# A trunk with fp32 weights split into a high and a low part: the split done per unit or per half unit

## The chip, the cores and the metric

The kernel runs on one core of a Trainium2 chip. The metric is the device time of one execution in microseconds: the median of repeated runs.

## The reference

`reference(x, ...)` is a small encoder trunk on x of 1 x 256 x 2048 in fp32, with two layers. Layer 0's mixer projects to 5120 columns and feeds a bidirectional gated linear recurrence (RG-LRU, 16 blocks, width-4 convolution, GeLU gate) and a dilated sliding-window attention with 16 heads; both are concatenated and projected back. Layer 1's mixer is a differential attention: projection to 6144 columns, two softmax maps per head, their difference weights the values, RMS norm per head, projection back. After each mixer comes a SwiGLU FFN, `(silu(h @ w_gate) * (h @ w_up)) @ w_down`, with 5632 hidden columns. Each sub-layer has an RMS norm ahead and one behind, `x = x + rms_norm(m, gain)`. All weights are fp32, 2048 rows or more, and are read once.

## The kernel before

*Matmuls.* The 256 tokens are two row tiles (t = 0, 1). All dense products are cut into **units**: a unit is a block of 512 x 512 of a weight, four k-tiles of 128 rows (KT = 4). There are 384 units, numbered u. To be near fp32 precision with the fast float32r matmul, weights and activations are split into a rounded high part and the remainder: each of the two products of a unit (`product`, L956) runs three passes of four matmuls: w_hi with h_hi, then w_lo with h_hi, then w_hi with h_lo (h the activations). A unit is 2 x 3 x 4 = 24 matmuls of 128 x 128 by 512 columns.

*The path of a weight.* SP issues one load of 1 MB into one of three `raw` buffers (`load`, L621), as soon as the subtraction that last read that buffer is done. ACT rounds it to `w_hi` (four buffers; `hi`, L728), DVE subtracts, `w_lo = raw - w_hi` (three buffers; `lo`, L1139). Two semaphores count units, `hi_done` and `lo_done`; PE waits for them at the head of passes 0 and 1 (L963, L971), and tells with `unit_done` that a unit's buffers are free. ACT's rounding runs 3 units ahead of PE (HI_LEAD), DVE's subtraction 2 (LO_LEAD). Unit 0 alone is loaded, rounded and subtracted in halves of two k-tiles, with semaphores of its own (first_landed, first_hi, first_lo), so that the kernel starts sooner.

*Order.* Every engine walks the same list of tasks (`Plan`, `run`, L247; hand-written orders at the boundaries between sub-layers, L288 and L314), each picking its own; an engine's queue is in order, so that a wait holds up what stands behind it. In the recurrence of layer 0, ACT (tanh, exp, sqrt) and DVE (scans and products) have the gates' work between roundings and subtractions. The FFN blocks 1 to 10 of each layer are a peeled body and a hardware loop of nine (`body` on each engine, L1120 for PE), 12 units each: there the counts that are waited for are computed from the loop's register `it`.

The SP queue also carries the recurrence's small weights (L651), parameters, gains and the input chunks of x.

Of the kernel before, what the change touches and what calls it, by code (L numbers as in the profile page):

```python
# [31 lines left out]
P = 128  # L32
# [400 lines left out]
def trunk(nc, x, norm_mix_pre, norm_mix_post, norm_ffn_pre, norm_ffn_post,  # L433
# [9 lines left out]
    with ExitStack() as ctx:  # L443
# [68 lines left out]
        pv = ctx.enter_context(nc.psum_tensor("pv", [P, 2, T], F32))  # L512


        landed = [sem(f"landed{i}") for i in range(RAW)]
        first_landed = sem("first_landed")
        first_hi = sem("first_hi")
        first_lo = sem("first_lo")
        hi_done = sem("hi_done")
        lo_done = sem("lo_done")  # L520
        half_done = sem("half_done")
# [55 lines left out]
        block = ctx.enter_context(nc.Block())  # L577


        def wait_event(eng, e):  # L580

            eng.wait_ge(tp_free[e % 2], e // 2 + 1)
# [30 lines left out]

        @block.sync
        def _(sp):
            def load_first(src):

                for ks, landed_half in ((slice(0, KT // 2), first_landed), (slice(KT // 2, KT), landed[0])):
                    sp.dma_start(raw[0][:, ks, :], src.rearrange("(k p) n -> p k n", p=P)[:, ks, :]).then_inc(landed_half, 16)

            def load(u, src, it=0):  # L621

                if u >= RAW:
                    sp.wait_ge(lo_done, u - RAW + 1 + 12 * it)
                sp.dma_start(raw[u % RAW][:, :, :], src.rearrange("(k p) n -> p k n", p=P)).then_inc(landed[u % RAW], 16)

            def input_chunk(c):

# [35 lines left out]
            def load_slot(slot):  # L664
                block = NF - 1 if slot.w == "down" else slot.kg
                rows = slice(block * KC, (block + 1) * KC)
                src = weights[slot.w][slot.layer][rows, slot.cb * KC:(slot.cb + 1) * KC]
                if slot.u:
                    load(slot.u, src)
                else:  # L670
                    input_chunk(0)
                    sp.dma_start(pre[:, :, :], pre_T).then_inc(pre_in, 16)
                    sp.dma_start(ident[:, :], identity).then_inc(ident_in, 16)
                    load_first(src)

            def task_of(task):
                if task.kind == "half" and task.t == 0 and task.passes[0] == 0:
# [38 lines left out]

        @block.scalar
        def _(act):
            def first_half():

                act.wait_ge(first_landed, 16)
                act.activation(w_hi[0][:, 0:KT // 2, :], raw[0][:, 0:KT // 2, :], ACT.Copy).then_inc(first_hi, 1)

            def rest_of_first():
                act.wait_ge(landed[0], 16)
                act.activation(w_hi[0][:, KT // 2:KT, :], raw[0][:, KT // 2:KT, :], ACT.Copy).then_inc(hi_done, 1)

            def hi(u, it=0):  # L728
                act.wait_ge(landed[u % RAW], 16 * (u // RAW + 1) + 16 * (12 // RAW) * it)
                if u >= HI:  # L730
                    act.wait_ge(unit_done, u - HI + 1 + 12 * it)
                act.activation(w_hi[u % HI][:, :, :], raw[u % RAW][:, :, :], ACT.Copy).then_inc(hi_done, 1)  # L732

            def square(task):

# [157 lines left out]
            def task_of(task):  # L893
                if task.kind == "T":
                    transposed(task)
                elif task.kind in ("square", "y_square"):
                    square(task)
                elif task.kind == "hi":
                    hi(task.u) if task.u else rest_of_first()
                elif task.kind == "first_half":  # L900
                    first_half()
                elif task.kind == "silu":
                    act.wait_ge(rstd_done, task.stat + 1)
                    silu(task.n, task.u, lambda t: act.wait_ge(tp_done, task.stage_free[t] + 1))
                elif task.kind == "par":
                    parameters(task.i)
                elif task.kind == "evac":
                    evac(task)
                elif task.kind == "s":
                    softmax(task)  # L910
                elif task.kind == "pt":
                    prob_transposed(task)
                elif task.kind == "pv":
                    values(task)
                elif task.kind == "rg_gates":
                    gates(task.i)
                elif task.kind == "rg_root":
                    root(task.i)
                elif task.kind == "rg_out":
                    recurrence_hi(task.i)  # L920
# [34 lines left out]
        def _(pe):  # L955
            def product(u, n, lhs, first, last, t, passes=(0, 3), it=0, high=None, low=None):  # L956

                hi_tile, lo_tile = w_hi[u % HI], w_lo[u % LO]
                for j in range(*passes):
                    a, w = ((1, hi_tile), (1, lo_tile), (0, hi_tile))[j]  # L960
                    if j == 0:
                        if u:
                            pe.wait_ge(hi_done, u + 1 + 12 * it)  # L963
                        else:
                            pe.wait_ge(first_hi, 1)
                        if first and n >= 2:
                            pe.wait_ge(acc_free[n % 2][t], n // 2 + 3 * it)
                        if high:
                            pe.wait_ge(*high)
                    elif j == 1:  # L970
                        if u:  # L971
                            pe.wait_ge(lo_done, u + 1 + 12 * it)
                        else:
                            pe.wait_ge(first_lo, 1)
                    elif low:
                        pe.wait_ge(*low)
                    for k in range(KT):
                        if u == 0 and k == KT // 2 and j < 2:
                            pe.wait_ge(lo_done if j else hi_done, 1)
                        mm = pe.matmul(acc[n % 2][t][:, :], operand(lhs, a, k, t), w[:, k, :],  # L980
                                       start=first and k == 0 and j == 0, stop=last and k == KT - 1 and j == 2)
                if passes[1] == 3:
                    mm.then_inc(unit_done if t else half_done, 1)
# [147 lines left out]

        @block.vector
        def _(dve):
            def lo_first(ks):

                dve.tensor_tensor(w_lo[0][:, ks, :], raw[0][:, ks, :], w_hi[0][:, ks, :].bitcast(F32),
                                  ALU.subtract).then_inc(lo_done if ks.start else first_lo, 1)

            def lo(u, it=0):  # L1139
                dve.wait_ge(hi_done, u + 1 + 12 * it)  # L1140
                if u >= LO:
                    dve.wait_ge(unit_done, u - LO + 1 + 12 * it)
                dve.tensor_tensor(w_lo[u % LO][:, :, :], raw[u % RAW][:, :, :],  # L1143
                                  w_hi[u % HI][:, :, :].bitcast(F32), ALU.subtract).then_inc(lo_done, 1)

            def operand_lo(e, m, hi_ap, lo_ap, it=0):
                dve.wait_ge(t_hi, m + 1 + NT * it)
# [150 lines left out]
            def task_of(task):  # L1298
# [9 lines left out]
                elif task.kind in ("rms_x", "rms_y"):  # L1308
                    mean(task)
                elif task.kind == "lo":  # L1310
                    if task.u:
                        lo(task.u)
                    else:
                        dve.wait_ge(hi_done, 1)
                        lo_first(slice(KT // 2, KT))
                elif task.kind == "first_half":
                    dve.wait_ge(first_hi, 1)
                    lo_first(slice(0, KT // 2))
                elif task.kind == "add_output":
                    slot = task.slot  # L1320
                    if slot.w == "ev_out" and slot.starts:
                        dve.wait_ge(rg_out, RG_OUT * AT)
                    add_output(slot.n, slot.u, slot.cb, slot.starts, task.t)
                elif task.kind == "difference":
                    difference(task)
                elif task.kind == "heads_scale":
                    heads_scale(task.g)
                elif task.kind == "gate_up":
                    gate_up(task.n, task.n + 1, task.u, lambda t: dve.wait_ge(tp_done, task.tok_free[t] + 1))
                elif task.kind == "s":  # L1330
                    softmax(task)
                elif task.kind == "heads":
                    heads_mean(task.g)
                elif task.kind == "pv":
                    values(task)
                elif task.kind == "rg_gates":
                    decay(task.i)
                elif task.kind == "rg_scan":
                    scan(task.i)
                elif task.kind == "rg_out":  # L1340
                    recurrence_lo(task.i)
                elif task.kind == "par":
                    parameters(task.i)
# [222 lines left out]
```

## Time and profile before

| | us |
|---|---|
| median of 3 runs | 2288.51 |
| lowest, highest | 2287.97, 2291.24 |
| the profiled execution | 2291.3 |
| its span (first to last instruction) | 2289.2 |
| PE busy | 2253.2 (98%) |
| DVE busy | 1313.1 (57%) |
| ACT busy | 1049.7 (46%) |
| 16 DMA engines, mean busy share | 54.9% |

Busy time is the time in which an engine runs an instruction, waits left out. L980 is the matmul line, with 9216 of PE's 10273 matmuls. A matmul is on record with 389 ns, but the next one starts 227 ns after it, since they are pipelined; distances between starts tell the pace. The line numbers are those of the kernel before.

### The profile page before, as it was taken

How to read it: one execution, taken by the hardware profiler on the slowest of the kernel's cores; microseconds unless marked ns; L12 is line 12 of the kernel's file. 1: busy time of each engine (PE TensorE's matmuls, PEld its weight loads, DVE VectorE, ACT ScalarE, POOL GpSimd, SP SyncE). 2: the span in 40 equal slices, each digit the busy share in tenths (PEclk: the TensorE clock that was granted, in tenths of full speed). 3: DMA queues.
4: the chain of work that ended last, by engine and by line, in shares of the span. 5: the costliest groups of instructions: out<-in, count | busy, mean ns of one | idle time of the engine just before them, and what ended most of it. 6: DMA issues, size and time to landing. Idle time of an engine off the chain costs nothing.

```text
span 2289.2 us, 27425 instructions
## 1 busy us (share of the span) xinstructions
PE 2253.2 (98%) x10273; PEld 1857.8 (81%) x10273; DVE 1313.1 (57%) x1416; ACT 1049.7 (46%) x1231; POOL 173.0 (8%) x200
## 2 busy tenths in 40 slices
PE   8999999999999999999999999999999999999997
PEld 6887888888888888888787778788888888888886
DVE  5567467654554555545745555776554555555546
ACT  6677545543433433334555555546333433333332
POOL 0841001000000000000121001010000000000002
PEclk9999999999999999999999999999999999999999
DMA  7555444655555556555464545456555655556552
GB/s 256 170 165 175 146 146 150 214 188 190 196 185 193 192 184 195 189 186 197 148 203 147 165 148 166 166 166 203 198 188 186 199 184 193 191 183 198 187 193 101
DMA packets 211400, 413.71 MB, mean 181 GB/s; under 512 B 12072, under 2 KB 12672, under 8 KB 210816
## 3 DMA queue, kind: packets, MB, share of 16 engines
q1 hardware_dynamic: 211328, 412.75, 54.9%
q8 instruction: 45, 0.74, 0.1%
q14 instruction: 27, 0.22, 0.0%
HBM read 410.63 MB, written 2.10 MB: 180 GB/s over the span
## 4 chain that ended last, share of the span: by engine, by line
PE 59%; issue 33%; DVE 4%; ACT 2%; DMA 1%; POOL 1%; SPq 0%; DVEq 0%; ACTq 0%; POOLq 0%
PE acc L980 54%; PE tp L994 2%; DVE w_lo L1143 2%; PE sc L1068 1%; DMA raw<-in_ev_w_in 1%; PE pv L1092 1%; PE sc L1064 1%; PE pv L1097 1%; DVE xs L1183 0%; DMA gq<-in_norm_ffn_post 0%; POOL yacc L1441 0%; ACT w_hi L732 0%; DVE h_lo L1156 0%; DVE gq L1287 0%; DVE tok L1263 0%
## 5 line engine op out<-in xcount | busy, mean ns | idle before, releaser
L1143 DVE TENSOR_TENSOR w_lo<-raw,w_hi 128x2048 fp32r<-128x2048 f32 x383 | 880.7, 2301 | 491.5 <-PE acc L980 464.5
L732 ACT ACTIVATE w_hi<-raw 128x2048 fp32r<-128x2048 f32 x383 | 734.4, 1918 | 757.4 <-PE acc L980 728.0
L980 PE MATMUL acc<-w_hi,h_hi 128*128 128x512 f32 x2240 | 612.8, 395 | 7.6 <-ACT h_hi L779 7.6
L980 PE MATMUL acc<-w_lo,h_hi 128*128 128x512 f32 x2240 | 600.7, 390 | 3.4 <-DVE w_lo L1143 3.4
L980 PE MATMUL acc<-w_hi,h_lo 128*128 128x512 f32 x2240 | 600.0, 390 | 1.5 <-DVE h_lo L1156 1.5
L980 PEld LDWEIGHTS acc<-w_lo,h_hi 128*128 128x128 f32 x2240 | 421.0, 188 | 93.3 <-DVE w_lo L1143 4.7
L980 PEld LDWEIGHTS acc<-w_hi,h_lo 128*128 128x128 f32 x2240 | 419.9, 188 | 90.7 <-DVE h_lo L1156 3.2
L980 PEld LDWEIGHTS acc<-w_hi,h_hi 128*128 128x128 f32 x2240 | 414.7, 188 | 92.1 <-issue 10.7
L1200 DVE TENSOR_TENSOR yacc<-acc,yacc 128x512 f32<-128x512 f32 x208 | 141.7, 687 | 167.6 <-PE acc L980 167.6
L980 PE MATMUL acc<-w_hi,y_hi 128*128 128x512 f32 x832 | 224.5, 392 | 0.7 <-ACT y_hi L933 0.7
L980 PE MATMUL acc<-w_lo,y_hi 128*128 128x512 f32 x832 | 222.6, 389 | 0.0
L980 PE MATMUL acc<-w_hi,y_lo 128*128 128x512 f32 x832 | 222.5, 389 | 0.0
L980 PEld LDWEIGHTS acc<-w_lo,y_hi 128*128 128x128 f32 x832 | 156.2, 188 | 32.7
L980 PEld LDWEIGHTS acc<-w_hi,y_lo 128*128 128x128 f32 x832 | 156.2, 188 | 32.6
L980 PEld LDWEIGHTS acc<-w_hi,y_hi 128*128 128x128 f32 x832 | 155.1, 188 | 32.9 <-issue 1.6
L1441 POOL TENSOR_TENSOR yacc<-yacc,gq 128x512 f32<-128x512 f32 x20 | 33.0, 1667 | 1539.9 <-ACT junk L748 1539.9
L840 ACT ACTIVATE probT<-tp 128x256 f32<-128x256 f32 (+1 forms) x48 | 21.9, 456 | 116.2 <-PE pv L1097 64.9
L933 ACT ACTIVATE y_hi<-tp 128x512 fp32r<-128x512 f32 x44 | 24.1, 596 | 87.8 <-PE tp L994 87.8
L1393 DVE SCALAR_TENSOR_TENSOR tok<-acc,small,stage 128x512 f32<-128x512 f32 x44 | 33.0, 751 | 52.8 <-PE acc L980 52.8
L927 ACT ACTIVATE stage<-acc,small 128x512 f32<-128x512 f32 x44 | 30.2, 690 | 56.6 <-PE acc L980 56.4
L1460 POOL TENSOR_TENSOR rot<-stage,ropes 128x128 f32<-128x128 f32 x24 | 21.3, 888 | 299.9 <-ACT stage L770 298.3
L828 ACT ACTIVATE prob<-sc,small 128x256 f32<-128x256 f32 x64 | 29.8, 470 | 25.7 <-DVE small L1218 25.6
(162 smaller groups left out, 1033.0 us busy)
## 6 DMA issues: line engine op xcount, KB each, us to landing
raw<-in_ffn_w_gate SPq DMA_DIRECT2D x88, 1024.0 KB, 5.2
raw<-in_ffn_w_up SPq DMA_DIRECT2D x88, 1024.0 KB, 5.2
raw<-in_ffn_w_down SPq DMA_DIRECT2D x88, 1024.0 KB, 5.0
raw<-in_od_w_in SPq DMA_DIRECT2D x48, 1024.0 KB, 5.1
raw<-in_ev_w_in SPq DMA_DIRECT2D x39, 1024.0 KB, 5.2
raw<-in_ev_w_out SPq DMA_DIRECT2D x16, 1024.0 KB, 5.0
raw<-in_od_w_out SPq DMA_DIRECT2D x16, 1024.0 KB, 5.0
xs<-in_x SPq DMA_DIRECT2D x4, 512.0 KB, 9.9
```

Of the source, the lines that this page charges most:

```text
L732: act.activation(w_hi[u % HI][:, :, :], raw[u % RAW][:, :, :], ACT.Copy).then_inc(hi_done, 1)
L828: ins = act.activation(prob[:, m, :], sc[:, m, :], ACT.Exp, scale=SCALE, bias=nmx[:, m:m + 1], accum_out=den[n % 2][:, m:m + 1])
L927: act.activation(stage[:, t, :], acc[n % 2][t][:, :], ACT.Silu, scale=rstd_x[:, t:t + 1]).then_inc(acc_free[n % 2][t], 1)
L933: act.activation(y_hi[:, 0:KT, t * P:(t + 1) * P], tp[t][:, :, :], ACT.Copy).then_inc(t_hi, 1)
L980: mm = pe.matmul(acc[n % 2][t][:, :], operand(lhs, a, k, t), w[:, k, :], start=first and k == 0 and j == 0, stop=last and k == KT - 1 and ...
L994: ins = pe.transpose(dst, src, ident[:, :])
L1064: mm = pe.matmul(sc[:, t, :], q[:, kt, t * P:(t + 1) * P], k[:, kt, task.i % 2, :], start=True, stop=True)
L1068: mm = pe.matmul(sc[:, :, :].rearrange("p m t -> p (m t)"), q[:, kt, t * P:(t + 1) * P], k[:, kt, :, :].rearrange("p m t -> p (m t)"), sta ...
L1143: dve.tensor_tensor(w_lo[u % LO][:, :, :], raw[u % RAW][:, :, :], w_hi[u % HI][:, :, :].bitcast(F32), ALU.subtract).then_inc(lo_done, 1)
L1200: dve.tensor_tensor(y, a, y, ALU.add).then_inc(acc_free[n % 2][t], 1)
L1393: dve.scalar_tensor_tensor(tok[:, t, :], acc[n_up % 2][t][:, :], rstd_x[:, t:t + 1], stage[:, t, :], ALU.mult, ALU.mult).then_inc(acc_free ...
L1441: pool.tensor_tensor(y, y, post_gain[:, cols], ALU.mult).then_inc(yg_pool, 1)
```

## The change

Every unit is now treated as unit 0 was. `load` issues two DMAs of 512 KB, one for each half of two k-tiles, each with a semaphore of its own per buffer and each behind its own wait for the subtraction of the same half three units ago. `hi` makes two ACT instructions of 128 x 1024, each behind its half's landing; `lo` two DVE instructions, each behind its half's rounding. `hi_done` and `lo_done` count halves, so that a unit adds 2 (24 in a loop body). PE waits at k = 0 and k = 2 of passes 0 and 1 instead of at the head of the pass. The semaphores of unit 0 are gone; the wait for `unit_done` stays one per unit, ahead of both halves. Cut to its core:

```diff
         pv = ctx.enter_context(nc.psum_tensor("pv", [P, 2, T], F32))
-        landed = [sem(f"landed{i}") for i in range(RAW)]
-        first_landed = sem("first_landed")
-        first_hi = sem("first_hi")
-        first_lo = sem("first_lo")
+        landed = [[sem(f"landed{i}{h}") for h in range(2)] for i in range(RAW)]
         hi_done = sem("hi_done")
         lo_done = sem("lo_done")
         half_done = sem("half_done")
...
         block = ctx.enter_context(nc.Block())
+        def tiles(h):
+            return slice(h * KT // 2, (h + 1) * KT // 2)
+
         def wait_event(eng, e):
             eng.wait_ge(tp_free[e % 2], e // 2 + 1)
...
         @block.sync
         def _(sp):
-            def load_first(src):
-
-                for ks, landed_half in ((slice(0, KT // 2), first_landed), (slice(KT // 2, KT), landed[0])):
-                    sp.dma_start(raw[0][:, ks, :], src.rearrange("(k p) n -> p k n", p=P)[:, ks, :]).then_inc(landed_half, 16)
-
             def load(u, src, it=0):
-                if u >= RAW:
-                    sp.wait_ge(lo_done, u - RAW + 1 + 12 * it)
-                sp.dma_start(raw[u % RAW][:, :, :], src.rearrange("(k p) n -> p k n", p=P)).then_inc(landed[u % RAW], 16)
+                for h in range(2):
+                    if u >= RAW:
+                        sp.wait_ge(lo_done, 2 * (u - RAW) + h + 1 + 24 * it)
+                    sp.dma_start(raw[u % RAW][:, tiles(h), :],
+                                 src.rearrange("(k p) n -> p k n", p=P)[:, tiles(h), :]).then_inc(landed[u % RAW][h], 16)
             def input_chunk(c):
...
                     input_chunk(0)
                     sp.dma_start(pre[:, :, :], pre_T).then_inc(pre_in, 16)
                     sp.dma_start(ident[:, :], identity).then_inc(ident_in, 16)
-                    load_first(src)
+                    load(0, src)
             def task_of(task):
                 if task.kind == "half" and task.t == 0 and task.passes[0] == 0:
...
         @block.scalar
         def _(act):
-            def first_half():
-
-                act.wait_ge(first_landed, 16)
-                act.activation(w_hi[0][:, 0:KT // 2, :], raw[0][:, 0:KT // 2, :], ACT.Copy).then_inc(first_hi, 1)
-
-            def rest_of_first():
-                act.wait_ge(landed[0], 16)
-                act.activation(w_hi[0][:, KT // 2:KT, :], raw[0][:, KT // 2:KT, :], ACT.Copy).then_inc(hi_done, 1)
+            def hi_half(u, h, it=0):
+                act.wait_ge(landed[u % RAW][h], 16 * (u // RAW + 1) + 16 * (12 // RAW) * it)
+                act.activation(w_hi[u % HI][:, tiles(h), :], raw[u % RAW][:, tiles(h), :], ACT.Copy).then_inc(hi_done, 1)
             def hi(u, it=0):
-                act.wait_ge(landed[u % RAW], 16 * (u // RAW + 1) + 16 * (12 // RAW) * it)
                 if u >= HI:
                     act.wait_ge(unit_done, u - HI + 1 + 12 * it)
-                act.activation(w_hi[u % HI][:, :, :], raw[u % RAW][:, :, :], ACT.Copy).then_inc(hi_done, 1)
+                for h in range(2):
+                    hi_half(u, h, it)
             def square(task):
...
                 elif task.kind in ("square", "y_square"):
                     square(task)
                 elif task.kind == "hi":
-                    hi(task.u) if task.u else rest_of_first()
+                    hi(task.u) if task.u else hi_half(0, 1)
                 elif task.kind == "first_half":
-                    first_half()
+                    hi_half(0, 0)
                 elif task.kind == "silu":
                     act.wait_ge(rstd_done, task.stat + 1)
                     silu(task.n, task.u, lambda t: act.wait_ge(tp_done, task.stage_free[t] + 1))
...
                 for j in range(*passes):
                     a, w = ((1, hi_tile), (1, lo_tile), (0, hi_tile))[j]
                     if j == 0:
-                        if u:
-                            pe.wait_ge(hi_done, u + 1 + 12 * it)
-                        else:
-                            pe.wait_ge(first_hi, 1)
                         if first and n >= 2:
                             pe.wait_ge(acc_free[n % 2][t], n // 2 + 3 * it)
                         if high:
                             pe.wait_ge(*high)
-                    elif j == 1:
-                        if u:
-                            pe.wait_ge(lo_done, u + 1 + 12 * it)
-                        else:
-                            pe.wait_ge(first_lo, 1)
-                    elif low:
+                    elif j == 2 and low:
                         pe.wait_ge(*low)
                     for k in range(KT):
-                        if u == 0 and k == KT // 2 and j < 2:
-                            pe.wait_ge(lo_done if j else hi_done, 1)
+                        if j < 2 and k % (KT // 2) == 0:
+                            pe.wait_ge((hi_done, lo_done)[j], 2 * u + k // (KT // 2) + 1 + 24 * it)
                         mm = pe.matmul(acc[n % 2][t][:, :], operand(lhs, a, k, t), w[:, k, :],
                                        start=first and k == 0 and j == 0, stop=last and k == KT - 1 and j == 2)
                 if passes[1] == 3:
...
         @block.vector
         def _(dve):
-            def lo_first(ks):
-
-                dve.tensor_tensor(w_lo[0][:, ks, :], raw[0][:, ks, :], w_hi[0][:, ks, :].bitcast(F32),
-                                  ALU.subtract).then_inc(lo_done if ks.start else first_lo, 1)
+            def lo_half(u, h, it=0):
+                dve.wait_ge(hi_done, 2 * u + h + 1 + 24 * it)
+                dve.tensor_tensor(w_lo[u % LO][:, tiles(h), :], raw[u % RAW][:, tiles(h), :],
+                                  w_hi[u % HI][:, tiles(h), :].bitcast(F32), ALU.subtract).then_inc(lo_done, 1)
             def lo(u, it=0):
-                dve.wait_ge(hi_done, u + 1 + 12 * it)
                 if u >= LO:
                     dve.wait_ge(unit_done, u - LO + 1 + 12 * it)
-                dve.tensor_tensor(w_lo[u % LO][:, :, :], raw[u % RAW][:, :, :],
-                                  w_hi[u % HI][:, :, :].bitcast(F32), ALU.subtract).then_inc(lo_done, 1)
+                for h in range(2):
+                    lo_half(u, h, it)
             def operand_lo(e, m, hi_ap, lo_ap, it=0):
                 dve.wait_ge(t_hi, m + 1 + NT * it)
...
                 elif task.kind in ("rms_x", "rms_y"):
                     mean(task)
                 elif task.kind == "lo":
-                    if task.u:
-                        lo(task.u)
-                    else:
-                        dve.wait_ge(hi_done, 1)
-                        lo_first(slice(KT // 2, KT))
+                    lo(task.u) if task.u else lo_half(0, 1)
                 elif task.kind == "first_half":
-                    dve.wait_ge(first_hi, 1)
-                    lo_first(slice(0, KT // 2))
+                    lo_half(0, 0)
                 elif task.kind == "add_output":
                     slot = task.slot
                     if slot.w == "ev_out" and slot.starts:
```

## Rows read from the trace of the kernel before

**Rows 1.** the page, part 1: busy us (share of the span), instructions of each engine.

```profile
PE 2253.2 (98%) x10273; PEld 1857.8 (81%) x10273; DVE 1313.1 (57%) x1416; ACT 1049.7 (46%) x1231; POOL 173.0 (8%) x200
```

**Rows 2.** a window of the FFN loop: us, busy PE, PEld, DVE, ACT, POOL, clock, DMA.

```profile
507.00:1103.00 596.00, 595.76 (x2666) 493.90 (x2664) 315.08 (x218) 228.07 (x146) 0.00 (x0) 1.00 0.58 190
```

**Rows 3.** PE's waits: for whom, us in total, times, longest us.

```profile
PE acc L980 <- DVE w_lo L1143: 3.4, 3, 1.9
PE sc L1064 <- DVE small L1211: 2.7, 1, 2.7
PE acc L980 <- DVE h_lo L1156: 1.5, 4, 0.4
```

**Rows 4.** timeline of PE in the loop: start us, us, what.

```profile
523.38 1.07 PE L980 MATMUL acc<-w_hi,h_hi 128*128 128x512 f32 x4
524.28 1.07 PE L980 MATMUL acc<-w_lo,h_hi 128*128 128x512 f32 x4
525.19 1.07 PE L980 MATMUL acc<-w_hi,h_lo 128*128 128x512 f32 x4
```

**Rows 5.** PE's sequencer on L963 and L967: duration ns min/median/max.

```profile
L963 PEldq ALU_OP  x198: 32/32/32, 508.4 to 2244.1; - x198
...
L967 PEldq EVENT_SEMAPHORE  x198: 51/51/51, 280.0 to 2246.8; - x198
```

**Rows 6.** timeline of DVE at the start and in the loop.

```profile
10.08 1.23 DVE L1136 TENSOR_TENSOR w_lo<-raw,w_hi 128x1024 fp32r<-128x1024 f32 x1 [10.08 <-ACT w_hi L722]
11.22 0.60 DVE L1156 SCALAR_TENSOR_TENSOR h_lo<-tp,pre,h_hi 128x128 fp32r<-128x128 f32 x2
...
17.23 2.29 DVE L1143 TENSOR_TENSOR w_lo<-raw,w_hi 128x2048 fp32r<-128x2048 f32 x1 [1.19 <-ACT w_hi L732]
19.44 0.60 DVE L1156 SCALAR_TENSOR_TENSOR h_lo<-tp,pre,h_hi 128x128 fp32r<-128x128 f32 x2
...
523.65 2.29 DVE L1143 TENSOR_TENSOR w_lo<-raw,w_hi 128x2048 fp32r<-128x2048 f32 x1 [3.22 <-PE acc L980]
```

**Rows 7.** timeline of ACT at the start.

```profile
8.99 1.06 ACT L722 ACTIVATE w_hi<-raw 128x1024 fp32r<-128x1024 f32 x1 [6.97 <-DMA raw<-in_ev_w_in]
9.95 0.61 ACT L779 ACTIVATE h_hi<-tp,pre 128x128 fp32r<-128x128 f32 x2
...
15.27 1.93 ACT L732 ACTIVATE w_hi<-raw 128x2048 fp32r<-128x2048 f32 x1
17.07 0.64 ACT L779 ACTIVATE h_hi<-tp,pre 128x128 fp32r<-128x128 f32 x2
```

**Rows 8.** the DMA table (last: us to landing); SP's issues on L625 (ns).

```profile
raw<-in_ffn_w_gate SPq DMA_DIRECT2D x88, 1024.0 KB, 5.2
...
L625 SPq DMA_DIRECT2D raw<-in_ffn_w_gate x88: 367/373/393, 366.6 to 2179.8; - x88
```

**Rows 9.** the chain of waits, 120 to 235 us: start us, us, what.

```profile
138.64 6.90 DMA raw<-in_ev_w_in
...
151.53 2.18 DVE w_lo L1143
...
213.82 2.18 DVE w_lo L1143
```

**Rows 10.** timelines of ACT and DVE around the late load.

```profile
145.56 1.92 ACT L732 ACTIVATE w_hi<-raw 128x2048 fp32r<-128x2048 f32 x1 [2.30 <-DMA raw<-in_ev_w_in]
...
146.98 0.75 DVE L1279 SCALAR_TENSOR_TENSOR yacc<-yacc,rgx 128x256 f32<-128x256 f32 x2
149.53 0.69 DVE L1282 SCALAR_TENSOR_TENSOR yacc<-yacc 128x512 f32<-128x512 f32 x1 [1.80 <-ACT yacc L887]
```

**Rows 11.** timeline of PE at the end of the recurrence.

```profile
193.15 1.21 PE L980 MATMUL acc<-w_lo,h_hi 128*128 128x512 f32 x4 [1.92 <-DVE w_lo L1143]
...
218.45 1.13 PE L1064 MATMUL sc<-gx,qT 128*128 128x256 f32 x4 [2.67 <-DVE small L1211]
...
222.40 1.40 PE L980 MATMUL acc<-w_lo,h_hi 128*128 128x512 f32 x4
```


## The prediction

> **What bounds the kernel now.** I read the page's busy shares first. PE, which runs the matmuls, is busy 2253.2 of the 2289.2 us of the span [rows 1]: whatever the change does to ACT, DVE or the transfers, the time can only fall by what PE waits, about 36 us, and can rise by anything that reaches PE. Next the windows: in the repeated FFN bodies PE is never idle; in 507 to 1103 it is busy 595.76 of 596 us, while DVE is busy 315 and ACT 228 [rows 2]. The two layers have 20 such bodies of 12 units of 24 matmuls, at 0.907 us for four [rows 4] 1306 us: more than half of the span has nothing to win. Then PE's own waits: the largest that touch the edited lines are 3.4 us in three waits for w_lo; one wait of 2.7 us for a softmax statistic; 1.5 us in four waits for h_lo [rows 3]. The reader should see how small these are beside 2289. Last the chain of waits, to see what those three causes hang on: from 138 to 218 us the chain runs through ACT and DVE, the recurrence's own instructions with w_lo subtractions between them, and through one load of raw [rows 9].
>
> **Part 1: more waits on PE.** Before, each product of a unit (384 units, two products) waits once for w_hi and once for w_lo: 4 waits a unit. After, each of these passes waits at k = 0 and at k = 2: 8 a unit, 4 x 384 = 1536 more, always long satisfied in the loops. The loop shows what a satisfied wait costs: the pass on w_hi,h_hi (it starts with a wait) starts at 523.38, the pass on w_lo (also a wait) at 524.28, the pass without one at 525.19: 0.90 and 0.91 us for four matmuls in either case, 227 ns a matmul [rows 4]. A wait costs nothing there, and neither do the register additions that compute the loop's counts: 32 ns each, 198 of them on that line, and 51 ns for a separate wait instruction [rows 5]; they are covered by the matmuls already queued. The new waits are half as far apart (two matmuls, 0.45 us, still far above 51 ns). I take 0. Upper bound, if this cover failed: 1536 x 0.051 = 78 us. Below nothing isn't possible, since a wait brings PE no work.
>
> **Part 2: the rounding and the subtraction in halves.** The kernel already does unit 0 in halves, so the trace has both sizes. ACT: a half starts at 8.99 and the next instruction at 9.95, 0.96 us; a whole one at 15.27, the next at 17.07, 1.80 us [rows 7]. Two halves are 1.92: +0.12 a unit. DVE: half 10.08 to 11.22, 1.14 us; whole 17.23 to 19.44, 2.21 us [rows 6]. Two halves are 2.28: +0.07 a unit. In the loops it is free: DVE sits idle 3.22 us before the subtraction [rows 6], and ACT is busy 38% [rows 2]. Outside, what counts is how many lie on the chain.
>
> The row shows that the instruction behind the half subtraction starts 1.14 us after it, before its 1.23 us are over [rows 6]. The Trainium skill ("VectorE: DVE Perf Modes", the sections on the errata and on the drain) has an fp32 tensor_tensor cost (N+151)/0.96 ns, and says that the next instruction doesn't start before the pipe is empty, so that many small instructions pay the fixed part each time. Its durations agree with the trace (1224 and 2291 by the formula, 1.23 and 2.29 us here), but by it each split would cost 0.157 and not 0.07 us, and the sum below would be about 1.2 us higher; the start-to-start times decide for 0.07.
>
> **Part 3: loads in halves.** Same bytes, rows of the same 2 KB, twice the issues. One issue takes SP 373 ns [rows 8], so a unit asks SP for 0.75 us of the 5.44 us it lasts (24 matmuls of 227 ns): nothing. A 1 MB load lands 5.2 us after its issue [rows 8]; a unit's raw slot is freed by its subtraction and not read again for over two units, so in the loops early halves win nothing. They can win where ACT waits for a landing and the chain goes through it: at 138.64 a load is issued when the subtraction ends, and takes 6.90 us [rows 9]; ACT stands idle 2.30 us for it, rounds 145.56 to 147.48, then does the recurrence's root, and DVE, which has stood idle 1.80 us, goes on at 149.53 [rows 10]. After the change the first half is issued 1.1 us earlier (one half subtraction) and the second at the same time with half the bytes. In the loop 190 GB/s pass [rows 2], but a load alone must be faster: 1 MB in at most 5.2 us, so 0.5 MB takes at least somewhat less. I take 1.3 us less (a quarter of 5.2). The second half is then there at 144.3; its rounding (0.96) ends at 145.3, against 147.4: 2.1 us earlier on ACT. DVE isn't free to use all of it: it ends its instructions of 146.98 at about 147.8, so the next can start at 147.9 and not 149.53: **-1.7 us**. Bounds: 0 (each half takes as long as a whole one and the rest of the chain is reached no earlier) and -2.4 (both halves there when ACT falls idle at 143.2).
>
> The trace has no lone 512 KB load. The Trainium skill ("DMA: Bandwidth & Descriptors", Bandwidth) advises transfers of at least 1 MiB for 75% of the peak, which speaks against halving them. If that rule bit here, the gain of -1.7 would be 0 and the sum +1.2; in the loops it could change nothing, PE has two more units in store.
>
> **What the chain gives back.** From 147 to 218 us it holds eight w_lo subtractions, the first at 151.53 and the last at 213.82 [rows 9], and two roundings: 8 x 0.07 + 2 x 0.12 = +0.8 us. Three more subtractions lie on it between 117 and 138: +0.2. At the three boundaries between layers' parts PE waits for h_lo behind a w_lo subtraction: 3 x 0.07 = +0.2.
>
> **PE's own three waits for w_lo.** The longest ends at 193.15 with the subtraction, 1.92 us [rows 11]. With halves two matmuls (0.45 us) can go ahead of the rest. But PE then comes earlier to 218.45, where it waits 2.67 us for the softmax statistic [rows 11], and this is set by the DVE and ACT chain, not by PE: what is won at 138, 193 and 204 us is waited out there. Gain 0, bound -1.3 (3 x 0.45). The same holds for PE's slow matmuls behind this wait: 222.40 for four, 1.40 us instead of 1.07 [rows 11]. The granted clock falls to its lower level, 1.2 GHz, for a few matmuls after the wait, about 1.1 us in all. The wait gets longer, not shorter, so I leave this cost as it is.
>
> **Sum.** -1.7 + 0.8 + 0.2 + 0.2 = -0.5 us. The profiled execution took 2291.3 us (span 2289.2 and 2.1 around it), 2.8 above the median of the three runs; it would become 2290.8. Against the median: 2288.5 - 0.5 = **2288.0 us**. With the bounds of parts 2 and 3 alone the sum lies between -2.5 (-2.4, -1.3 and +1.2) and +2.4 (no gain of the load, 0.14 instead of 0.07 for 14 subtractions, and 0.12 more for two roundings): 2286.0 to 2290.9.
>
> **Rivals.**
> *The recurrence stretch gives back its idle time.* PE waits 3.4 us for w_lo, 2.7 us for the statistic and 0.2 us behind it, 6.3 us in all, between 138 and 220, and 1.1 us go to the slow matmuls [rows 3, 11]. If earlier halves loosen the whole chain (DVE may begin when half of w_hi is there; loads start a microsecond earlier each time), all could go: 2288.5 - 7.4 = 2281.1. For it: all waits there hang on one chain. Against it: only one load on that chain was late; the rest is ACT's and DVE's own work, which the change makes longer.
> *Nothing moves:* landings of halves are no earlier in effect, and +0.07 is hidden too: 2288.5. It differs from the forecast by less than can be measured.
> *Slower: waits inside a pass aren't hidden.* A wait at k = 2 comes in the middle of a pass, where in this kernel only unit 0 has one, at the start, with nothing to compare. If the weight load that carries it can't be taken ahead, or the register additions come too thick in the loops, each costs something: at 32 ns 49 us (2337), at 51 ns 78 us (2367). It decides from 3 ns a wait on, as 1536 x 3 ns is 4.6 us. Against it: the loads that carry waits now are taken ahead like the others, to within 0.01 us a pass [rows 4].
> *Slower by ACT's and DVE's fixed costs alone:* everything at the upper bound, the load's gain gone and the boundaries paying for roundings too (3 x 0.2): +3.0, 2291.5. By itself this stays below the threshold.
>
> **Chances.** A measurement of this kernel can tell 0.2%, 4.6 us, from no change. Forecast and "nothing moves" together with the fixed-cost case: 0.80, of which the forecast 0.45, nothing moves 0.22, fixed costs 0.13. Idle time given back: 0.12, of which 0.11 over the threshold. Waits not hidden: 0.08. So faster 0.11, same 0.81, slower 0.08. The range: the sum's own bounds, 2286.0 to 2290.9, widened to about half of the first rival (2283) and to the fixed-cost case (2292); the waits that aren't hidden stay outside.
>
> **What would show it.** In the profile after: 770-odd instructions on ACT and on DVE for w_hi and w_lo, each near 1.06 and 1.22 us, ACT about 80 and DVE about 55 us busier (part 2). Passes in the loop still 0.90 to 0.91 us apart, also those with two waits, and PE's matmuls two and three of a pass no further apart than 227 ns (part 1); 0.92 or more would prove me wrong and give the third rival. ACT's wait for raw near 145 us gone or under 1 us, DVE's next recurrence step before 149.5 (part 3). PE's wait near 193 us shorter, that near 218 longer, and its end at 217.5 to 218.5. If PE's wait at 218 shrinks too, the first rival is right. DMA issues of 512 KB that land under 5.2 us after issue confirm the load's term; 5 us or more would take it away.

## The result and the profile after

| | before | after |
|---|---|---|
| median of 20 runs, us | 2288.47 | 2292.53 |
| lowest to highest | 2286.86 to 2291.24 | 2290.64 to 2293.61 |
| profiled execution, its span | 2291.3, 2289.2 | 2292.96, 2290.9 |

The ratio is 1.0015, 95% interval 1.0009 to 1.0021: slower by 4.1 us, where -0.5 was forecast, and just outside the range (2292.0). It lies under the 4.6 us that I had set as the threshold. The two profiled executions differ by 1.7 us only, since the one before was 2.8 us longer than its median.

The page of the changed kernel, part 1, and its window of the FFN loop (columns as in [rows 2]):

```profile
PE 2253.9 (98%) x10273; PEld 1858.3 (81%) x10273; DVE 1345.4 (59%) x1799; ACT 1084.2 (47%) x1614; POOL 166.2 (7%) x200
```

```profile
507.00:1103.00 596.00, 595.70 (x2666) 493.87 (x2665) 322.80 (x325) 237.72 (x255) 0.00 (x0) 1.00 0.59 190
```

PE's busy time is that of [rows 1] within 0.7 us, and in the loop it is busy all the time, as in [rows 2]. So the loss is neither work of PE nor in the loops. It is in PE's waits; these answer to [rows 3]:

```profile
PE acc L963 <- DVE h_lo L1138: 4.8, 3, 1.6
...
PE sc L1047 <- DVE small L1193: 3.3, 1, 3.3
PE acc L963 <- DVE w_lo L1119: 1.8, 5, 0.4
```

The wait for w_lo fell from 3.4 to 1.8 us, and the one for the softmax statistic rose from 2.7 to 3.3. Most of that fall isn't the change's: a second profile of the kernel before (e8, below) has 2.0 us of waits for w_lo. The wait for h_lo rose from 1.5 to 4.8: three waits of 1.6 us, where there were three of 0.4 and one of 0.3. They stand at the three boundaries between sub-layers, near 394, 1130 and 1548 us. There h_lo, the low part of the activations, is written by DVE behind a w_lo subtraction in its queue, so PE's third pass, which reads h_lo, waits for the subtraction too. The timelines of DVE and POOL at the first of them, in the kernel before:

```profile
389.35 3.38 DVE L1143 TENSOR_TENSOR w_lo<-raw,w_hi 128x2048 fp32r<-128x2048 f32 x1
392.65 0.68 DVE L1200 TENSOR_TENSOR yacc<-acc,yacc 128x512 f32<-128x512 f32 x1
393.25 0.60 DVE L1156 SCALAR_TENSOR_TENSOR h_lo<-tp,pre,h_hi 128x128 fp32r<-128x128 f32 x2
...
389.01 4.88 POOL L1441 TENSOR_TENSOR yacc<-yacc,gq 128x512 f32<-128x512 f32 x2 [1.43 <-ACT junk L748]
```

and after, each instruction by itself (the first two are the halves):

```profile
387.84 2.31 DVE L1119 TENSOR_TENSOR w_lo<-raw,w_hi 128x1024 fp32r<-128x1024 f32 x1
...
390.07 2.30 DVE L1119 TENSOR_TENSOR w_lo<-raw,w_hi 128x1024 fp32r<-128x1024 f32 x1
...
387.50 1.57 POOL L1418 TENSOR_TENSOR yacc<-yacc,gq 128x512 f32<-128x512 f32 x1 [1.36 <-ACT junk L740]
...
389.03 2.25 POOL L1418 TENSOR_TENSOR yacc<-yacc,gq 128x512 f32<-128x512 f32 x1
```

Read them in the order of time. POOL (the GpSimd engine) multiplies by the post-norm gain, 1.30 us for 128x512 when nothing is in its way. Before, the whole subtraction starts while POOL's first multiplication is at work and takes 3.38 us instead of 2.29 [rows 6], 1.1 too long. After, the first half takes 2.31 us instead of 1.22, and ends at 390.15; POOL's second multiplication, begun at 389.03, takes 2.25 and ends at 391.28, about one multiplication later than the half; the second half begins at 390.07, takes 2.30 and ends at 392.37, again about 1.1 us later than that. They take turns by instruction (tested below). The whole subtraction met one POOL instruction and held off the other; two halves meet both. PE's row at this place says what it costs (before in the first fence, after in the second):

```profile
394.42 1.20 PE L980 MATMUL acc<-w_hi,h_lo 128*128 128x512 f32 x4 [0.41 <-DVE h_lo L1156]
```

```profile
394.06 1.21 PE L963 MATMUL acc<-w_hi,h_lo 128*128 128x512 f32 x4 [1.59 <-DVE h_lo L1138]
```

Three times 1.59 - 0.41 is 3.5 us.

The same meeting happens elsewhere, with other POOL instructions: outside the boundaries 14 halves of the changed kernel take 0.1 to 0.55 us longer than 1.22 us (most of them between 60 and 140 us), and five whole subtractions of the kernel before 0.1 to 0.6 us longer than 2.29. What these cost can't be told from the scatter of that part (see e8).

### The profile page after: what moved, and what is told of

It is laid out like the page before. It is cut to its first block, busy times and chain, and to the rows that moved or that the text cites. A ratio compares the mean times of both kernels' runs of the same rounds, so it can differ in the third digit from the quotient of the medians.

```text
span 2290.9 us, 29654 instructions
## 1 busy us (share of the span) xinstructions
PE 2253.9 (98%) x10273; PEld 1858.3 (81%) x10273; DVE 1345.4 (59%) x1799; ACT 1084.2 (47%) x1614; POOL 166.2 (7%) x200
## 4 chain that ended last, share of the span: by engine, by line
PE 60%; issue 33%; DVE 4%; ACT 2%; POOL 1%; DMA 1%; SPq 0%; DVEq 0%; ACTq 0%; POOLq 0%
PE acc L963 54%; PE tp L977 2%; DVE w_lo L1119 2%; PE sc L1051 1%; PE sc L1047 1%; PE pv L1075 1%; ACT w_hi L718 1%; PE pv L1080 1%; DVE xs L1165 0%; DMA gq<-in_norm_ffn_post 0%; POOL yacc L1418 0%; DMA raw<-in_ev_w_in 0%; ACT stage L762 0%; DVE gq L1269 0%; ACT kz L874 0%
## 5 line engine op out<-in xcount | busy, mean ns | idle before, releaser
L1119 DVE TENSOR_TENSOR w_lo<-raw,w_hi 128x1024 fp32r<-128x1024 f32 x768 | 915.2, 1233 | 485.0 <-PE acc L963 462.9
L718 ACT ACTIVATE w_hi<-raw 128x1024 fp32r<-128x1024 f32 x768 | 771.8, 1054 | 737.5 <-PE acc L963 715.0
L963 PE MATMUL acc<-w_hi,h_hi 128*128 128x512 f32 x2240 | 612.3, 395 | 6.5 <-ACT h_hi L771 3.7
L963 PE MATMUL acc<-w_hi,h_lo 128*128 128x512 f32 x2240 | 600.3, 390 | 4.8 <-DVE h_lo L1138 4.8
L963 PE MATMUL acc<-w_lo,h_hi 128*128 128x512 f32 x2240 | 601.4, 390 | 1.8 <-DVE w_lo L1119 1.8
L963 PEld LDWEIGHTS acc<-w_hi,h_lo 128*128 128x128 f32 x2240 | 420.5, 188 | 93.8 <-DVE h_lo L1138 6.1
L963 PEld LDWEIGHTS acc<-w_lo,h_hi 128*128 128x128 f32 x2240 | 420.4, 188 | 92.3 <-DVE w_lo L1119 4.1
L963 PEld LDWEIGHTS acc<-w_hi,h_hi 128*128 128x128 f32 x2240 | 414.6, 188 | 90.8 <-issue 5.3
L963 PE MATMUL acc<-w_hi,y_hi 128*128 128x512 f32 x832 | 224.5, 392 | 0.6 <-issue 0.6
L963 PE MATMUL acc<-w_lo,y_hi 128*128 128x512 f32 x832 | 222.6, 389 | 0.0
L963 PE MATMUL acc<-w_hi,y_lo 128*128 128x512 f32 x832 | 222.5, 389 | 0.0
L963 PEld LDWEIGHTS acc<-w_lo,y_hi 128*128 128x128 f32 x832 | 156.2, 188 | 32.7
L963 PEld LDWEIGHTS acc<-w_hi,y_lo 128*128 128x128 f32 x832 | 156.2, 188 | 32.5
L963 PEld LDWEIGHTS acc<-w_hi,y_hi 128*128 128x128 f32 x832 | 155.1, 188 | 32.9 <-issue 1.5
```

The lines of the kernel that those rows point to most:

```text
L718: act.activation(w_hi[u % HI][:, tiles(h), :], raw[u % RAW][:, tiles(h), :], ACT.Copy).then_inc(hi_done, 1)
L1119: dve.tensor_tensor(w_lo[u % LO][:, tiles(h), :], raw[u % RAW][:, tiles(h), :], w_hi[u % HI][:, tiles(h), :].bitcast(F32), ALU.subtract).t ...
```

## The experiments

The stretch from PE's first matmul of unit 56 (391.93 before, 390.38 after) to the end of the span holds all three boundaries. In two profiles of the same kernel it repeats to 0.1 us (before and e8, e3 and e3b), which no whole run does, so it stands beside the median in this table. "Ratio" is to the kernel before measured together with the run: 2288.47 us beside the changed kernel, 2289.05 to 2289.16 beside the others.

| run | median us | ratio (95%) | unit 56 to end, us | against before |
|---|---|---|---|---|
| before, beside the experiments | 2289.05 to 2289.16 | | 1897.31 | |
| after | 2292.53 | 1.0015 (1.0009 to 1.0021) | 1900.51 | +3.2 |
| e1_whole3 | 2288.32 | 0.9998 (0.9989 to 1.0007) | 1897.09 | -0.2 |
| e2_halves3 | 2291.78 | 1.0012 (1.0003 to 1.0021) | 1900.83 | +3.5 |
| e3_before_pool256 | 2286.70 | 0.9988 (0.9979 to 0.9997) | 1895.13 | -2.2 |
| e4_after_pool256 | 2288.35 | 0.9995 (0.9986 to 1.0004) | 1896.05 | -1.3 |
| e5_loads | 2288.59 | 0.9999 (0.9990 to 1.0008) | 1897.32 | 0.0 |
| e6_halves_whole_loads | 2292.78 | 1.0016 (1.0007 to 1.0025) | 1900.54 | +3.2 |
| e7_waits | 2289.27 | 1.0001 (0.9992 to 1.0010) | 1897.36 | 0.0 |
| e8_before_again | 2289.65 (one) | | 1897.26 | -0.1 |
| e11_quarters3 | 2292.66 | 1.0015 (1.0006 to 1.0024) | 1901.25 | +3.9 |
| e12_whole3_pool256 | 2286.84 | 0.9991 (0.9982 to 1.0000) | 1894.89 | -2.4 |
| e3b_before_pool256 | 2286.59 | 0.9989 (0.9980 to 0.9998) | 1895.16 | -2.1 |

My theory after the result, P: DVE and POOL take turns by instruction, and halves meet one POOL instruction more. Rivals: F, the fixed cost of the added instructions; S, a shared bandwidth, by which both only slow down while they overlap.

**e1_whole3**: the changed kernel with one subtraction per boundary whole.

```diff
-    tasks += [update(1, 0), lo(u + 5), add(s3, 1), ...
+    tasks += [update(1, 0), Task("lo", u=u + 5, i=1), add(s3, 1), ...
 # in lo, for this task:
+                    dve.wait_ge(hi_done, 2 * u + 2)
+                    dve.tensor_tensor(w_lo[u % LO][:, :, :], raw[u % RAW][:, :, :],
+                                      w_hi[u % HI][:, :, :].bitcast(F32), ALU.subtract).then_inc(lo_done, 2)
```

> The changed kernel, but at the three boundaries (about 388, 1124 and 1542 us) the one subtraction that meets POOL's two gain multiplications is again one instruction of 128x2048. Theory P (DVE and POOL take turns, one instruction at a time, and each DVE instruction waits for the POOL instruction that is running): that subtraction takes 3.4 us instead of 4.5, PE's wait for h_lo falls from 1.6 to 0.4 us, and the kernel is 3 x 1.15 = 3.5 us faster than the changed one: 0.9 to 1.0 of what was lost. Rival F (the loss is the fixed cost of all the extra instructions, or the rounding that comes in halves): PE's wait stays near 1.6 us and the time within 1 us of the changed kernel's.

Three pairs of halves out of 384, made whole, undo the whole loss, to within the interval. DVE's row again takes the 3.4 us of the kernel before:

```profile
386.58 3.37 DVE L1127 TENSOR_TENSOR w_lo<-raw,w_hi 128x2048 fp32r<-128x2048 f32 x1
```

**e2_halves3**: the mirror image, the kernel before with only these three split.

```diff
-                dve.tensor_tensor(w_lo[u % LO][:, :, :], ...).then_inc(lo_done, 1)
+                for ks in (slice(0, KT // 2), slice(KT // 2, KT)) if halves else (slice(0, KT),):
+                    ins = dve.tensor_tensor(w_lo[u % LO][:, ks, :], raw[u % RAW][:, ks, :],
+                                            w_hi[u % HI][:, ks, :].bitcast(F32), ALU.subtract)
+                ins.then_inc(lo_done, 1)
```

> The kernel before with one edit: the same three subtractions as two instructions of 128x1024; loads, roundings, waits of PE and the other 381 subtractions as before. P: DVE takes 4.5 us for these instead of 3.4, PE's wait for h_lo rises from 0.4 to 1.6 us, and the kernel is 3.5 us slower (1.0015). F: 3 x 0.07 = 0.2 us, no change.

Three added instructions bring +3.5 us in the stretch and 1.0012 (2.7 us) in the ratio, whose interval holds 3.5. F would have them cost 0.2 and falls. DVE and then PE:

```profile
386.42 4.53 DVE L1144 TENSOR_TENSOR w_lo<-raw,w_hi 128x1024 fp32r<-128x1024 f32 x2
```

```profile
392.65 1.20 PE L980 MATMUL acc<-w_hi,h_lo 128*128 128x512 f32 x4 [1.56 <-DVE h_lo L1158]
```

**e3_before_pool256 and e3b**: the kernel before; POOL's gains in two instructions each.

```diff
-                pool.tensor_tensor(y, y, post_gain[:, cols], ALU.mult).then_inc(yg_pool, 1)
+                gain = post_gain[:, cols]
+                for c0 in (0, KC // 2):
+                    ins = pool.tensor_tensor(y[:, c0:c0 + KC // 2], y[:, c0:c0 + KC // 2], gain[:, c0:c0 + KC // 2], ALU.mult)
+                ins.then_inc(yg_pool, 1)
```

> The kernel before, but POOL's gain multiplications are issued as two instructions of 128x256 each. P: the whole subtraction near 389 us waits only for the rest of a POOL instruction of about 0.65 us instead of 1.3, so it takes about 2.8 instead of 3.4 us; PE's wait for h_lo (0.4) goes, three times: -1.2 us or a little more. Rival S (the two engines share a bandwidth and slow each other down for as long as both are at work): same bytes on both, the subtraction stays at 3.4 us, no change.

> The kernel before with POOL's gains in two instructions of 128x256, once more beside the two others: 2286.7 to 2287.5, ratio 0.9990 with an interval below 1.

The same bytes on both engines, and the subtraction is 0.55 us shorter: S, which wanted no change, falls.

```profile
387.22 2.83 DVE L1143 TENSOR_TENSOR w_lo<-raw,w_hi 128x2048 fp32r<-128x2048 f32 x1
```

PE's wait for h_lo is gone at all three boundaries. The stretch is 2.2 us shorter, more than the 1.2 us of the waits: 0.54 at each of the three boundaries (the four matmuls behind a wait also take 1.20 us on record, not 1.07), and 0.55 at the end, where the time from PE's last matmul to the end of the span is 11.7 instead of 12.2 us. A DVE instruction that this end hangs on, on yacc and xs at 2274.16 us, meets a POOL multiplication, too: it takes 1.78 us in the kernel before and 1.22 in e3. Both runs have an interval below 1: this is a version that beats the kernel before by 2.4 to 2.6 us, small as that is, and the changed one by more.

**e4_after_pool256**: the same edit of POOL on the changed kernel.

> The changed kernel with POOL's gain multiplications in two instructions of 128x256 each. P: each half subtraction waits up to 0.55 us instead of 1.1, the pair takes about 3.4 instead of 4.5 us, PE's wait for h_lo falls from 1.6 to 0.5 us, three times: -3.3 us against the changed kernel. S: the pair stays at 4.5 us, no change.

```profile
387.70 3.42 DVE L1119 TENSOR_TENSOR w_lo<-raw,w_hi 128x1024 fp32r<-128x1024 f32 x2
```

As P wants: two halves, each behind a POOL instruction of half the length, 3.42 us (3.4 expected; 4.53 with POOL's long ones), PE's waits for h_lo 0.5 each. The median is 4.2 us under that of the changed kernel (measured another time), the stretch 4.5 us shorter, where 3.3 was expected: 3.3 of it are the three boundaries, 1.1 lie behind PE's last matmul, twice what e3 wins there.

**e5_loads**: the kernel before, loads in halves alone.

```diff
+                for ks in (slice(0, KT // 2), slice(KT // 2, KT)):
+                    sp.dma_start(raw[u % RAW][:, ks, :], ...[:, ks, :]).then_inc(landed[u % RAW], 16)
 # in hi: wait for 32 a load
```

> The kernel before with each 1 MB load as two of 512 KB issued together; roundings, subtractions and PE's waits whole. If halved loads cost transfer rate, ACT's waits for raw grow and the time with them, by a few us; I expect landings of the second half at 5.2 us after its issue as for the whole load, and no change within 1 us.

**e6_halves_whole_loads**: the changed kernel, loads of 1 MB.

```diff
-                    sp.dma_start(raw[u % RAW][:, tiles(h), :], ...).then_inc(landed[u % RAW][h], 16)
+                for h, ks in ((0, tiles(0)), (1, tiles(1))) if u == 0 else ((1, slice(0, KT)),):
+                    sp.dma_start(raw[u % RAW][:, ks, :], ...).then_inc(landed[u % RAW][h], 16)
```

> The changed kernel with whole loads of 1 MB again (roundings, subtractions and waits in halves). If the loss is all at the three boundaries, it stays: 1.0015 against the kernel before, boundaries 1.15 us longer each. If the halved loads carried a gain or a loss in the recurrence, the stretch from 138 to 220 us differs from the changed kernel's by more than 0.5 us.

The two together: halved loads do nothing in the stretch in either kernel (0.0 and 0.0), and nothing in the time that can be measured. Nor in the recurrence: from PE's first matmul of unit 2 (near 26 us) to the end of its wait for the statistic near 218 us, e6 took 190.9 us and the changed kernel 191.1, closer than the 0.5 us that I had set as a sign. In the DMA table a 512 KB load lands sooner than a 1 MB one, 4.4 us after its issue against 5.1 (e5 first, e6 second):

```profile
raw<-in_ffn_w_gate SPq DMA_DIRECT2D x176, 512.0 KB, 4.4
```

```profile
raw<-in_ffn_w_gate SPq DMA_DIRECT2D x88, 1024.0 KB, 5.1
```

0.7 us sooner, without effect on the time. The median mixes the two halves that e5 issues together: the first landed 3.8 us after its issue, the second 4.6, where I had expected 5.2 (in the changed kernel 3.7 and 4.7).

**e7_waits**: the kernel before with PE's added waits alone.

```diff
-                        if u == 0 and k == KT // 2 and j < 2:
-                            pe.wait_ge(lo_done if j else hi_done, 1)
+                        if k == KT // 2 and j < 2:
+                            pe.wait_ge(lo_done if j else hi_done, u + 1 + 12 * it)
```

> The kernel before with PE's added waits alone: in passes 0 and 1 also a wait at k = 2, for the count that was reached at k = 0. My part 1 says: passes of the loop stay 0.907 us apart, no change (within 1 us). The rival says at least 3 ns a wait, 4.6 us.

PE's timeline in its loop, passes with two waits each in lines 1, 2 and 4:

```profile
523.27 1.07 PE L980 MATMUL acc<-w_hi,h_hi 128*128 128x512 f32 x4
524.18 1.07 PE L980 MATMUL acc<-w_lo,h_hi 128*128 128x512 f32 x4
525.09 1.07 PE L980 MATMUL acc<-w_hi,h_lo 128*128 128x512 f32 x4
526.00 1.07 PE L980 MATMUL acc<-w_hi,h_hi 128*128 128x512 f32 x4
```

0.91 us apart, as in [rows 4]. The 1536 waits more cost nothing that shows: 0.0 us in the stretch, and the whole run's interval ends at +2.3 us, half of what 3 ns a wait would be.

**e8_before_again**: the kernel before, a second profile.

> The kernel before once more, for a second profile. If the late load near 138 us (6.90 us, ACT idle 2.30) was an accident of the one profiled execution, it lands in 5.1 to 5.6 us here, ACT idles under 1 us, and the stretch from unit 2 to unit 33 is 1.5 to 2 us shorter than the 203.2 us of the first profile. If it belongs to the kernel, it is there again. At the three boundaries PE waits 0.4 us for h_lo as in the first profile.

The load near 138 us landed 5.4 us after its issue, and ACT waited 0.83 us, not 2.30 [rows 10]:

```profile
142.93 1.93 ACT L732 ACTIVATE w_hi<-raw 128x2048 fp32r<-128x2048 f32 x1 [0.83 <-DMA raw<-in_ev_w_in]
```

```profile
190.54 1.20 PE L980 MATMUL acc<-w_lo,h_hi 128*128 128x512 f32 x4 [0.50 <-DVE w_lo L1143]
```

PE's wait for w_lo near 191 us, 1.92 in [rows 11], is 0.50. So the late load doesn't belong to every execution. But it isn't an accident of a single one either. Eight of the profiles kept here are of kernels with whole roundings and subtractions at this place. In four (before, e7, e5, e3b) the load lands 6.0 to 6.9 us after its issue and ACT waits 1.7 to 2.3 us for it; in four (e8, e2, e11, e3) it lands after 5.3 to 5.5 us and ACT waits 0.7 to 0.9. (Of e5's two parts the second is meant.) From unit 2 to the end of the wait for the statistic the first four took 191.5 to 192.3 us and the others 190.5 to 190.8. The five with halves (after, e1, e4, e6, e12) took 190.5 to 191.1. So it fits that halves take away what a late load costs, 0.7 us or more, and win nothing in an execution without one; no run shows this for the median. What makes the load late is open.

The stretch from unit 2 to 33 was only 0.5 us shorter in e8, not 1.5 to 2 (up to unit 30 it was 1.5 us shorter). The difference goes with the granted clock, which was at its lower level (1.2 GHz, 0.5 in the profile) twice as long after the wait for the statistic, 6.8 us against 3.4. From the end of this wait to unit 56 the five profiles with 6.8 us (e8, e7, e5, e6, e4) took 174.4 to 174.5 us, the eight with 3.4 us 173.1 to 173.5. Both kinds are there with and without halves. Over nine profiles of kernels with POOL's gains whole, unit 2 to unit 56 took 363.7 to 366.0 us with whole subtractions (before, e8, e5, e7, e2, e11) and 363.7 to 365.3 with halves (after, e1, e6). Whatever halves do in the recurrence is smaller than this scatter.

**e11_quarters3**: as e2, with four instructions of 128x512.

```diff
-                for ks in (slice(0, KT // 2), slice(KT // 2, KT)) if halves else (slice(0, KT),):
+                for ks in [slice(k, k + 1) for k in range(KT)] if halves else (slice(0, KT),):
```

> The kernel before with the three boundary subtractions in four instructions of 128x512 each (POOL's gains whole, two instructions of 128x512). Theory P, in turns: DVE waits once for each POOL instruction that still comes in between, and POOL has two, so two of the four quarters wait about 1.1 us and the others don't: the four take 4.5 to 4.8 us in all, as two halves did, and the kernel is 3.5 to 4.3 us slower than before. Rival C (each DVE instruction pays about 1.1 us for a busy POOL, however many POOL instructions there are): 2.5 + 4 x 1.1 = 6.9 us, PE waits 3.8 us for h_lo, 3 x 3.4 = 10 us slower.

```profile
387.69 4.65 DVE L1144 TENSOR_TENSOR w_lo<-raw,w_hi 128x512 fp32r<-128x512 f32 x4
```

4.65 us, with two POOL instructions about. One by one, the quarters take 1.78, 1.75, 0.68 and 0.68 us: two wait about 1.1 us, two don't. So it is not C, a toll on each DVE instruction (6.9 us): DVE loses its turn once for each POOL instruction that is at work or ready when it is to begin.

**e12_whole3_pool256**: e1 with POOL's gains in two instructions each.

> The changed kernel with the three boundary subtractions whole and POOL's gains in two instructions of 128x256: PE's wait for h_lo at the boundaries is 0 as in the kernel before with halved gains. Expected 2287.0: -1.3 us against the same without halved gains (2288.3), equal to the kernel before with halved gains within 1 us, since halves elsewhere bring nothing in the typical execution.

2286.84 us against e3b's 2286.59, measured together: halves of loads, roundings and subtractions everywhere but at the boundaries bring nothing that can be measured.

## Why the prediction was wrong

- **What bounds the kernel**: right. PE is as busy as before, the loops did not move.
- **Part 1, waits on PE, 0**: right, shown by e7.
- **Part 2, +0.07 us for each subtraction**: the step that failed, at "3 x 0.07 = +0.2" for the boundaries; measured there are 3 x 1.18 = 3.5 us in PE's waits, 3.2 us (changed kernel) and 3.5 us (e2) in the stretch. The 0.07 was read near 10 and 17 us, where POOL does nothing. At the boundaries POOL does, and the row was in the trace before: the subtraction at 389.35 takes 3.38 us, and the chain of waits gave it 3.29. I took the 2.29 us median for all of them and did not ask why three of 383 were 1.1 us longer. Had I, with POOL's two multiplications beside it, +1.1 us a boundary could have been the forecast. Away from POOL the 0.07 fits: DVE is busy 32.3 us longer, 3.5 of them at the boundaries, the rest 0.075 us for each of 384. ACT is busy 34.5 us longer, 0.09 a unit, where I took 0.12; the 55 and 80 us that I named as signs were too high.
- **Part 3, -1.7 us from the late load**: wrong in size for a typical execution. The mechanism did what I said: halves landed 3.7 and 4.7 us after their issue in the loop, ACT's wait near 145 us is gone, and DVE's next recurrence step stands at 147.6 us. But the 2.30 us of waiting that the term was read from are those of a late load, which four of eight profiles have. The profiled execution took 2.8 us longer than the median; I noted this and did not ask what in the profile it was. In the profiles without a late load (e8, e2, e11, e3) this part takes no longer than with halves.
- **PE's waits for w_lo won and given back**: right in kind. Against e8, which has no late load, 2.0 us became 1.8, and the wait for the statistic 3.3 instead of 2.7 us.
- **Rivals**: none named the cause. Idle time given back did not happen. Waits not hidden: excluded by e7. The fixed costs alone: excluded by e2, where three added instructions did it. My -0.5 without the -1.7 is +1.2, and with 3.5 in place of 0.2 it is +4.5, against +4.1 measured. That this is so near is partly luck: +1.0 of it, the recurrence's own (0.8 + 0.2), no run shows. With the boundaries mended e1 is at 0.9998 of the kernel before (0.9989 to 1.0007), and e12 0.25 us above e3b.

The page "GPSIMD Engine Reference" of the Trainium skill (section Key points) says that GpSimd shares its SBUF interfaces with VectorE and contends with VectorE instructions that have two SBUF inputs. The traces agree: both instructions here have two. And the addition at 392.65 us, whose acc lies in PSUM, takes no longer than elsewhere (0.68 us, 0.69 on average), though POOL's second multiplication lasts until 393.89. That the turns are whole instructions, so that splitting one of them costs a turn, is shown by the runs (e2, e3, e4, e11). Had I weighed that page instead of the one on the drain, it would have pointed at the place.

## What to carry to other kernels

Before an elementwise instruction on DVE is split, look at each instance of it for one that takes longer than the median, and at what POOL does there: where the two meet, n pieces meet up to n POOL instructions, and each costs the rest of that one. The remedy is on the other side: keep DVE's instruction whole on the critical stretch and cut POOL's into small ones (2.4 to 2.6 us here, for four more instructions a boundary and eight at the end). And when a profiled execution is longer than the median, take a second profile and find out which stretch is longer and by how much, before a gain is read from it.

## What was not expected of the hardware

- DVE and POOL took turns by whole instructions where both read two SBUF operands: 128x1024 took 2.31 us instead of 1.22 while a 1.30 us POOL instruction was at work; 128x2048 took 3.38 instead of 2.29, and 2.83 with POOL instructions half as long. In the same way POOL's second instruction waited for the DVE one, 3.34 us for the whole and 2.25 for the half (it takes 1.30 alone).
- A second wait in the middle of a pass of four matmuls, 0.45 us from the first, did not move the start of any pass in the loop (0.91 us, as before).
- One load of 1 MB landed in 6.9 us in one execution and in 5.4 in another, at the same place of the same kernel; beside these, in 6.3 and 6.5 us in e7 and e3b, in 5.3 to 5.5 in e2, e11 and e3.
- After the same wait of PE, of about 2.7 or 3.3 us, the granted clock was at its lower level for 3.4 us in eight executions and for 6.8 us in five, whichever the kernel; the longer one cost about 1.2 us.
